# First layer's scaled copy of x transposed moved behind Pool's other loads of the layer

## What is computed

```python
h = rms_norm(x, mix_norm[l])
proj = h @ in_proj[l]                       # + vres_down in layer 1
p_rwkv = token_shift(proj[..., :RWKV_COLS], shift_mu[l])   # p + (prev - p) * mu
p_diff = proj[..., RWKV_COLS:IN_COLS]       # no token shift
y_rwkv, v_l = rwkv7_time_mix(p_rwkv, ...)   # needs all of p_rwkv
y_diff = diff_attention(p_diff, ...)
x = x + jnp.concatenate([y_rwkv, y_diff], -1) @ out_proj[l]
```

## Time and profile before

| | us |
|---|---|
| median of three executions | 1905.78 |
| the profiled execution | 1910.01 |
| its span in the trace | 1908.2 |
| PE busy | 1833.6 (96%) |
| DVE busy | 1494.2 (78%) |
| ACT busy | 1173.2 (61%) |
| Pool busy | 75.9 (4%) |

### The profile page before, as it was taken

The page is one execution under the profiler, slowest core; times in us unless marked ns, Lnnn a source line. Parts: engine busy times, 40 slices in busy tenths (PEclk is TensorE's granted clock), DMA queues, the critical chain, the costliest instruction groups (busy, mean ns, idle before and its releaser), DMA issues.

```text
span 1908.2 us, 31578 instructions
## 1 busy us (share of the span) xinstructions
PE 1833.6 (96%) x10589; PEld 1423.0 (75%) x10589; DVE 1494.2 (78%) x2051; ACT 1173.2 (61%) x1576; POOL 75.9 (4%) x111
## 2 busy tenths in 40 slices
PE   7999998999989999988999999999999999999998
PEld 5555577888875555677888888888888888888886
DVE  5854776655577557765999999989999999999997
ACT  5332454555544124453888787787787788877875
POOL 3200000000030000001200000000000000000000
PEclk9999999999998999998999999999999999999999
DMA  8531262666553322434999999999999999999993
GB/s 257 166 98 60 81 210 89 200 190 188 185 156 110 119 64 78 158 108 167 338 382 337 362 354 355 368 337 364 348 355 371 352 344 384 336 358 350 360 367 144
DMA packets 224172, 474.51 MB, mean 249 GB/s; under 512 B 16712, under 2 KB 41432, under 8 KB 223792
## 3 DMA queue, kind: packets, MB, share of 16 engines
q1 hardware_dynamic: 219600, 459.08, 68.3%
q0 software_dynamic: 3488, 12.87, 2.1%
q10 hardware_dynamic: 960, 1.10, 0.2%
HBM read 468.25 MB, written 1.05 MB: 246 GB/s over the span
## 4 chain that ended last, share of the span: by engine, by line
PE 54%; DVE 1%; issue 0%; ACT 0%; DVEq 0%
PE psum L474 17%; PE psum L476 16%; PE psum L475 16%; PE psum L1014 2%; PE psum L1061 1%; PE psum L1025 0%; PE psum L1026 0%; PE psum L873 0%; PE psum L885 0%; PE psum L498 0%; ACT hN L1294 0%; PE psum L583 0%; ACT SH L1486 0%; PE psum L1106 0%; DVE x L2244 0%
## 5 line engine op out<-in xcount | busy, mean ns | idle before, releaser
L474 PE MATMUL psum<-w_hi,h_hi 128*128 128x512 f32 (+1 forms) x1552 | 613.4, 395 | 20.4 <-DVE w_lo L428 17.3
L476 PE MATMUL psum<-w_hi,h_lo 128*128 128x512 f32 (+1 forms) x1552 | 607.0, 391 | 0.0
L475 PE MATMUL psum<-w_lo,h_hi 128*128 128x512 f32 (+1 forms) x1552 | 606.6, 391 | 0.0
L474 PEld LDWEIGHTS psum<-w_hi,h_hi 128*128 128x128 f32 x1552 | 294.7, 190 | 90.3 <-DVE w_lo L428 17.9
L476 PEld LDWEIGHTS psum<-w_hi,h_lo 128*128 128x128 f32 x1552 | 294.7, 190 | 62.3
L475 PEld LDWEIGHTS psum<-w_lo,h_hi 128*128 128x128 f32 x1552 | 294.9, 190 | 59.7 <-issue 0.5
L428 DVE SCALAR_TENSOR_TENSOR w_lo<-ring,col,w_hi 128x512 fp32r<-128x512 f32 (+1 forms) x184 | 132.0, 763 | 70.5 <-ACT w_hi L414 69.9
L444 DVE TENSOR_TENSOR w_lo<-ring,w_hi 128x1024 fp32r<-128x1024 f32 x144 | 172.3, 1221 | 7.7 <-ACT w_hi L440 3.2
L440 ACT ACTIVATE w_hi<-ring 128x1024 fp32r<-128x1024 f32 x144 | 151.8, 1060 | 41.0 <-PE psum L476 40.9
L414 ACT ACTIVATE w_hi<-ring,col 128x512 fp32r<-128x512 f32 (+1 forms) x184 | 118.9, 697 | 90.8 <-PE psum L476 84.4
L444 DVE TENSOR_TENSOR w_lo<-dproj,w_hi 128x1024 fp32r<-128x1024 f32 x120 | 145.9, 1223 | 17.2 <-ACT w_hi L440 13.6
(11 more groups left out here) (327 smaller groups left out, 2465.1 us busy)
## 6 DMA issues: line engine op xcount, KB each, us to landing
ring<-in_expert_w_gu SPq DMA_DIRECT2D x128, 512.0 KB, 5.4
SH<-in_expert_w_gu SPq DMA_DIRECT2D x120, 512.0 KB, 5.8
proj<-in_expert_w_gu SPq DMA_DIRECT2D x104, 512.0 KB, 6.2
dproj<-in_expert_w_gu SPq DMA_DIRECT2D x72, 512.0 KB, 5.8
dproj<-in_expert_w_down SPq DMA_DIRECT2D x72, 512.0 KB, 5.1
ring<-in_expert_w_down SPq DMA_DIRECT2D x64, 512.0 KB, 5.2
ring<-in_in_proj SPq DMA_DIRECT2D x48, 512.0 KB, 4.1
ring<-in_dense_w_gu SPq DMA_DIRECT2D x88, 256.0 KB, 3.1
```

The source lines that it names most:

```text
L474: pe.matmul(o, h[0], w[0], start=start, stop=False, skip_group_check=True)
L475: pe.matmul(o, h[0], w[1], start=False, stop=False, skip_group_check=True)
L476: return pe.matmul(o, h[1], w[0], start=False, stop=stop, skip_group_check=True)
```

## The change

In layer 0 `gained_x(0)` goes from between the LORA shift and the R shift to behind the V shift and the four small loads that follow it, just ahead of the wait for `rk_read`. Layer 1 is unchanged.

```diff
@@ -1242,8 +1242,6 @@
                 if l == 0:
                     pool.dma_start(vec[:, VEC_PARTS[0]], vecs[0, VEC_PARTS[0]].partition_broadcast(P)).then_inc(vec_in[0], 16)
                 shift_in(l, LORA_)
-                if l == 0:
-                    gained_x(l)
                 if l:
                     shift_in(l, VR_)
                 shift_in(l, R_)
@@ -1256,6 +1254,7 @@
                         pool.dma_start(w_, s).then_inc(side_in, 16)
                     for q in range(DEPTH):
                         pool.dma_start(scol[:, q:q + 1], vecs[q:q + 1, a:a + w].rearrange("l p -> p l")).then_inc(scol_in, 16)
+                    gained_x(l)
                 pool.wait_ge(rk_read, l + 1)
                 pool.dma_start(mem_raw, mem_in[0].rearrange("(t p) d -> p t d", p=P)).then_inc(mem_in_s, 16)
```

## The result

The changed kernel takes 1925.7 us, the median of six executions (1921.0 to 1927.8), beside 1907.2 for the kernel before (1903.6 to 1908.8, six). The ratio is 1.0095, with a 95% interval of 1.0084 to 1.0106: 16 to 20 us slower, about 18. The forecast was +14.5 and 1920.3; the measured time lies inside the stated range, near its upper end, and 5.4 us above the forecast itself.

A forecast was written before the change was run, and what follows sets the result against it. PE was taken to bound the kernel. The copy's end at 89.2 minus line 541's old start at 76.69, plus 2.0 for the clock, gave +14.5 us on the median 1905.8: 1920.3 us, range 1913 to 1926.

The forecast's parts named there:

- What bounds the kernel, and the mechanism: PE, busy 96% of the span, sets the end; the change trades a DVE gain before 53 us against a PE wait.
- Part 1: Without the copy between 37 and 53 us DVE runs undisturbed, so PE arrives 5.2 us sooner, at 71.5; ends 0 and 6.0.
- PE keeps up: Between 37 and 53 us PE's blocks take about 2.7 us each at full clock, so block 13 is finished by 53.
- Part 2: Pool's earlier issues cost PE nothing; the copy starts at 73.6 us, takes 15.6 and ends at 89.2.
- like the old place: At the new place DVE is busy 14.51 of 18 us, so the copy was given its old length, 15.6 us.
- Part 3: PE, ready at 71.5 us, waits for the copy until 89.2: 17.7 us idle in front of line 541.
- The hidden parts: Behind PE's wait, DVE's slowing of about 6 us and the memory tokens' load at about 91 cost nothing.
- Part 4: After the idle time PE's first matmuls of line 541 run at a lower clock, costing 2.0 us; ends 1.0 and 2.7.
- Quick copy: Rival: the copy at its new place takes only layer 1's 12.2 us, 6.0 gained before: +9.3, 1915.1 us; chance 0.10.
- DVE not freed: Rival: DVE's slow rows at the old place have another source, so nothing is gained: +19.7, 1925.5 us; chance 0.10.
- Full exclusion: Rival: DVE's two-input instructions stop Pool entirely at the new place, the copy taking 22.1 us: +21.0, 1926.8 us; chance 0.05.
- Taken up later: Rival: PE's 19.4 us of idle time behind line 541 absorbs the wait, at the extreme 1900.9 us; chance 0.05.

The follow-up runs named there:

- half_new: Changed kernel with only the first half of layer 0's copy made; PE waits for that half, other products read x: 1913.8 us, ratio 1.0033.
- free_none: Kernel before without layer 0's copy; PE's line 541 products there read x itself and don't wait: 1899.4 us, ratio 0.9968.
- free_new: Changed kernel, copy at the new place, but PE's line 541 products in layer 0 read x itself and don't wait: 1901.1 us, ratio 0.9968.
- warm: Changed kernel with 21 extra matmuls on PE ahead of its wait for the copy: 1925.1 us, ratio 1.0097 to the kernel before.
- early: Kernel before with layer 0's copy moved ahead of the key shift: 1909.1 us, ratio 1.0016.
- after_R: Kernel before with layer 0's copy moved behind the R shift and its vec load, ahead of the V shift: 1907.8 us, ratio 1.0013.
- after: First profile of the changed kernel itself, layer 0's copy at the new place: median 1925.7 us, ratio 1.0095 to the kernel before.
- free_old: Kernel before, copy at its old place, but PE's line 541 products in layer 0 read x itself and don't wait: 1907.2 us, ratio 1.0004.
- warm2: Second run of the changed kernel with 21 extra matmuls on PE ahead of its wait for the copy: 1923.4 us, ratio 1.0084.

## Why the prediction came out as it did

The time lies in the range, and the steps happened as told; but the forecast's own band of 3 us, to which the prediction gave 0.70, missed by 2.4. Of the 5.4 us, 1.4 are the median of the kernel before, 1905.8 from three executions and 1907.2 from six; of the other 4.0 the terms below account for 1.9, and the rest isn't resolved.

**What bounds the kernel, and the mechanism**: right. A wait put in front of line 541 goes to the end one for one (`half_new`), and nothing behind takes it up (the table).

**Part 1, the gain of 5.2 us**: right in kind and about right in size. Line 1732 (1731 after) ended at 47.2 instead of 53.7; 0.9 of that is an earlier start, and the stretch itself took 10.3 instead of 16.0, 5.7 less. `free_none` and `free_new` are both 6.1 us faster by the ratio. "PE keeps up" reckoned with the full clock, although the rows of before show 0.79 for this stretch; no reason was given that the clock would rise, and it did, to 1.00. PE reached the wait at 68.9, 71.3 and 68.6 us in the three changed traces, where 71.5 was forecast; the traces with the old timing start line 541 at 76.7 and 74.2.

**Part 2, Pool's queue**: right for the issues; the copy started at 71.0, 73.4 and 70.7 (forecast 73.6). The length of the copy was the term mis-sized: 15.6 taken, 17.7 measured, because "like the old place" wasn't quite so. At 17.7 us it came close to the 18 that the prediction had named as a sign of being wrong. At the old place nine of DVE's twelve instructions were of 0.7 us (line 428's, of 512 columns, and the LORA mix); at the new place its wide instructions are nine of 1.22 us. That Pool waits longer behind longer instructions fits its first rows (2.32 and 1.84, 1.33 and 1.31 before), but no run varied that size alone, so this stays argued.

**Part 3, the wait**: 17.7 forecast, 19.9 measured; the 2.2 us are those of the copy's length. The hidden parts stayed hidden: `free_new` shows it for DVE's slowed share, and the memory load was issued at 89.06.

**Part 4, the clock**: 2.0 forecast, 2.6 to 3.1 in the three changed traces from line 541 to line 679 (29.8, 30.3 and 29.8 us against 27.2).

With the measured terms the sum is 19.9 of wait, less 6.1 gained, plus 2.6 for the clock: +16.4, against 16.0 to 20.2 measured, and 16.8 at line 679 in the traces. The 1 to 2 us to the medians' 18 aren't resolved, and that the clock's 2.6 reach the end is not shown (`warm`).

**The rivals.** Quick copy: refuted (17.7, not 12.2). DVE not freed: refuted by `free_none`, although its total, 1925.5, is the closest of all to the median; the right number would have come from a wrong reason. Full exclusion: refuted in size, 17.7 against 22.1 us. The Trainium skill's lock rule (page "SBUF — State Buffer"; it stands in the section "SBUF: two separate sides", not in the one that the prediction names) predicted the direction in which the copy's length missed, and the trace stands between my value and the rule's. Taken up later: refuted by the table.

## What to carry to other kernels

A helper's work with a large lead may look free, and still cost through the port or engine it disturbs; before moving it, ask both whom it slows and by when its product is wanted, since every microsecond past the lead is one of the kernel. Here the lead was 24 us; the copy's end moved 36 us later (52.6 to 88.8) and PE came 8 us sooner (76.7 to 68.9), 44 in all, and the difference is the wait of 20. What helped here was not another place for the work but less of it on the contended engine: a part went to one that idled there.

When a shift of work is costed, take the length of a contended instruction from its neighbours at the new place, not from the old place alone. And two single profiles can differ by several microseconds from their medians in opposite directions: cut both at common marks before reading their difference.

## What the runs showed of the hardware

An instruction of DVE over only two columns took 0.65 us beside Pool's two-input instructions (`early`), against 0.16 alone: and two instructions of 16 columns took 2.21 us (`after_R`) against 0.39. This contention hits chains of tiny steps. Pool's sum of 128x512 fp32 took 1.26 us in `early` while DVE idled, and 2.32 beside full-width instructions of DVE (`after`). PE's clock fell to its lower level behind waits of 1.92 and 1.74 us in the trace before and of 2.14 and 1.82 in `free_old`, and behind 1.89 us of idle time in `warm2` but not in `warm`, so the same code can meet either level.
